# Projection products of 386 columns instead of 392 in a hybrid SSD / DeltaNet / MoE layer

## The reference

```
h = rmsnorm(x, lp['norm1_w']) * (1 + sc1) + sh1
proj = h @ lp['w_in']
xbc = jax.nn.silu(centred_dwconv(xbc, lp['conv_ssd_w'], lp['conv_ssd_b']))    # padding 2 on both sides
qkv = jax.nn.silu(centred_dwconv(qkv, lp['conv_dn_w'], lp['conv_dn_b']))
```

## Time and profile before

| | |
|---|---|
| median of three runs | 1172.71 us (1168.2 to 1173.03) |
| the profiled execution | 1171.63 us |
| its span, first to last instruction | 1169.7 us |
| mean granted TensorE clock | 0.961 |
| TensorE busy | 1037.3 us, 89% |
| VectorE, ScalarE, GpSimd busy | 514.2, 293.9, 228.9 us |
| L734, all 1176 products, in the chain of waits | 18.1% of the span |

### The profile page before, as it was taken

One profiled execution on the slowest core, in us unless ns is written; L12 is line 12 of the kernel. 1 busy time (PEld: TensorE's weight loads), 2 busy tenths in 40 slices (PEclk: granted clock), 3 DMA queues, 4 the chain that ended last, 5 costly groups with the idle time before them and its releaser, 6 DMA issues.

```text
span 1169.7 us, 21559 instructions
## 1 busy us (share of the span) xinstructions
PE 1037.3 (89%) x9055; PEld 679.7 (58%) x9055; DVE 514.2 (44%) x1013; ACT 293.9 (25%) x663; POOL 228.9 (20%) x180
## 2 busy tenths in 40 slices
PE   2799999998898788888999799998988989999895
PEld 1599999997554577778555454443433433444342
DVE  0675776213874455667410433442332333333344
ACT  2432333434452334344100330110111111111112
POOL 0554555561141322322000200000000000000000
PEclk9899999999996999999999899999998999999998
DMA  9742423416052600100412589999999999999993
GB/s 358 255 144 73 144 97 120 144 73 243 10 207 87 253 4 4 40 3 22 144 46 99 214 307 387 407 425 427 425 426 426 424 426 426 426 425 425 426 426 126
DMA packets 54909, 279.11 MB, mean 239 GB/s; under 512 B 6712, under 2 KB 14136, under 8 KB 36016
## 3 DMA queue, kind: packets, MB, share of 16 engines
q1 hardware_dynamic: 51296, 270.12, 57.4%
q0 software_dynamic: 3536, 7.85, 1.8%
HBM read 278.12 MB, written 4.72 MB: 242 GB/s over the span
## 4 chain that ended last, share of the span: by engine, by line
PE 60%; DMA 23%; DVE 10%; ACT 3%; issue 2%; POOL 1%; SPq 1%; DVEq 0%; ACTq 0%
DMA ring_b<-in_w_up 18%; PE ps L734 18%; PE ps L1173 13%; PE ps L1003 7%; DMA ring_a<-in_w_gate 4%; PE ps L1191 2%; PE ps L675 2%; DVE temp L1793 1%; PE ps L824 1%; DMA kv<-in_pos_t 1%; PE ps L926 1%; PE ps L952 1%; PE ps L979 1%; PE ps L804 1%; PE ps L833 1%
## 5 line engine op out<-in xcount | busy, mean ns | idle before, releaser
L734 PE MATMUL ps<-h_hi,w_split 128*128 128x392 f32 x784 | 204.3, 342 | 0.6 <-POOL w_split L584 0.6
L1173 PE MATMUL ps<-ring_b,temp 128*64 128x512 f32 x512 | 124.3, 642 | 28.9 <-DMA ring_b<-in_w_up 28.9
L734 PEld LDWEIGHTS ps<-h_hi,w_split 128*128 128x128 f32 x784 | 143.6, 188 | 3.5 <-issue 2.5
L734 PE MATMUL ps<-h_lo,w_split 128*128 128x392 f32 x392 | 134.2, 342 | 0.0
L584 POOL TENSOR_TENSOR w_split<-ring_a,w_split 128x1024 fp32r<-128x1024 f32 x46 | 114.5, 2489 | 92.3 <-ACT w_split L1309 92.3
L1173 PE MATMUL ps<-ring_a,temp 128*64 128x512 f32 x512 | 114.6, 599 | 7.8 <-DMA ring_a<-in_w_gate 6.9
L1191 PE MATMUL ps<-mix,temp 128*64 128x512 f32 x256 | 112.9, 594 | 2.5 <-issue 0.7
L1191 PE MATMUL ps<-kv,temp 128*64 128x512 f32 x256 | 113.3, 596 | 0.0
L2020 DVE SCALAR_TENSOR_TENSOR temp<-temp,silu_c,ps 128x512 f32<-128x512 f32 x16 | 12.0, 747 | 227.5 <-PE ps L1173 227.5
L1173 PEld LDWEIGHTS ps<-ring_b,temp 128*64 128x64 f32 x512 | 43.7, 147 | 107.9 <-issue 107.9
L1173 PEld LDWEIGHTS ps<-ring_a,temp 128*64 128x64 f32 x512 | 42.6, 139 | 76.7 <-issue 76.5
(11 more groups left out here) (329 smaller groups left out, 1652.3 us busy)
## 6 DMA issues: line engine op xcount, KB each, us to landing
ring_b<-in_w_up SPq DMA_DIRECT2D x30, 2048.0 KB, 18.1
ring_a<-in_w_gate SPq DMA_DIRECT2D x28, 2048.0 KB, 17.3
mix<-in_w_down SPq DMA_DIRECT2D x32, 1024.0 KB, 16.4
kv<-in_w_down SPq DMA_DIRECT2D x32, 1024.0 KB, 18.5
ring_a<-in_w_in SPq DMA_DIRECT2D x11, 2048.0 KB, 7.7
ring_a<-in_w_ada SPq DMA_DIRECT2D x6, 2048.0 KB, 11.4
ring_b<-in_w_ada SPq DMA_DIRECT2D x6, 2048.0 KB, 19.1
ring_a<-in_w_gate SPq DMA_DIRECT2D x16, 512.0 KB, 6.9
```

The lines of the kernel that those rows point to most:

```text
L734: last = nc.tensor.matmul(ps[:, 2 + n % 3, 0:ROW], w[:, k, :], h[:, k, :], start=(k == 0 and x == 0), stop=(k == KD - 1 and x == 2))
L1173: last = nc.tensor.matmul(ps[64 * e:64 * e + 64, 2 + n, :], xg_t[:, k, 64 * e:64 * e + 64], slots[2 * n + e][:, k, :], start=(k == 0), sto ...
```

## The change

The four zero columns between the two sequences become two: the convolution of a sequence needs two zeros behind it and two ahead of it, and the gap's two serve both. The outer zeros, two on each side, are no columns of the product any more: VectorE writes them once into the three PSUM banks, at the columns 0:2 and 388:390, and the products go to the columns 2:388. The convolution reads 386 shifted columns, j to j + 386. `conv_acc` and `ROW_SEGS` follow. The first sequence now begins at column 0 of a row block and the second at 130.

```
-ROW = TOK + 8
-W5 = TOK + 4
-ROW_SEGS = ((2, SEQ + 2), (SEQ + 6, TOK + 6))
+GAP = 2
+ROW = TOK + GAP
+ROW_SEGS = ((0, SEQ), (SEQ + GAP, ROW))
+OUT0, OUT_COLS = GAP, ROW + 2 * GAP
...
-        conv_acc = carve(784, 2, 388)
+        conv_acc = carve(784, 2, ROW)
...
-                last = nc.tensor.matmul(ps[:, 2, 0:ROW], w_split[:, 0, w, k, :], h[:, k, :], ...)
+                last = nc.tensor.matmul(ps[:, 2, OUT0:OUT0 + ROW], w_split[:, 0, w, k, :], h[:, k, :], ...)
...
-                last = nc.tensor.matmul(ps[:, 2 + n % 3, 0:ROW], w[:, k, :], h[:, k, :],
+                last = nc.tensor.matmul(ps[:, 2 + n % 3, OUT0:OUT0 + ROW], w[:, k, :], h[:, k, :],
...
-                nc.scalar.activation(dest[:, 0:SEQ], conv_acc[:, i % 2, 0:SEQ], ACT.Silu)
-                nc.scalar.activation(dest[:, SEQ:TOK], conv_acc[:, i % 2, SEQ + 4:TOK + 4], ACT.Silu).then_inc(conv_out, 1)
+                for (lo, hi), (a, b) in zip(SEGS, ROW_SEGS):
+                    last = nc.scalar.activation(dest[:, lo:hi], conv_acc[:, i % 2, a:b], ACT.Silu)
+                last.then_inc(conv_out, 1)
...
-                            last = nc.scalar.activation(mix[:, i, lo:hi], ps[:, bank, a:b], ACT.Silu)
+                            last = nc.scalar.activation(mix[:, i, lo:hi], ps[:, bank, OUT0 + a:OUT0 + b], ACT.Silu)
...
+            for lo in (0, OUT_COLS - GAP):
+                V.memset(ps[:, 2:5, lo:lo + GAP], 0.0)
             V.memset(silu_c[:, :, :], 0.0).then_inc(silu_zero, 1)
...
-            for lo, hi in ((0, 2), (SEQ + 2, SEQ + 6), (TOK + 6, ROW)):
-                last = V.memset(h1_t[:, :, lo:hi], 0.0)
-            link(last)
+            link(V.memset(h1_t[:, :, SEQ:SEQ + GAP], 0.0))
...
-                link(V.tensor_scalar(c_acc, row[:, 0:W5], col("conv_w", CONV_W * i), col("conv_b", i), ALU.mult, ALU.add))
+                link(V.tensor_scalar(c_acc, row[:, 0:ROW], col("conv_w", CONV_W * i), col("conv_b", i), ALU.mult, ALU.add))
...
-                    ins = V.scalar_tensor_tensor(c_acc, row[:, j:j + W5], col("conv_w", CONV_W * i + j), c_acc, ALU.mult, ALU.add)
+                    ins = V.scalar_tensor_tensor(c_acc, row[:, j:j + ROW], col("conv_w", CONV_W * i + j), c_acc, ALU.mult, ALU.add)
```

More of the change, by code:

```diff
@@ L720, in first_block @@
                         pe.wait_ge(made, k + 1)
-                        last = nc.tensor.matmul(ps[:, 2, 0:ROW], w_split[:, 0, w, k, :], h[:, k, :], start=(x == 0 and k == 0), stop=(x == 2 and k == KD - 1))
+                        last = nc.tensor.matmul(ps[:, 2, OUT0:OUT0 + ROW], w_split[:, 0, w, k, :], h[:, k, :], start=(x == 0 and k == 0), stop=(x == 2 and k == KD - 1))
                 last.then_inc(block_mm, 1)
@@ L1339, in _ @@
                         if 2 <= i <= 4:
-                            last = nc.scalar.copy(mix[:, i, lo:hi], ps[:, bank, a:b])
+                            last = nc.scalar.copy(mix[:, i, lo:hi], ps[:, bank, OUT0 + a:OUT0 + b])
                         else:
-                            last = nc.scalar.activation(mix[:, i, lo:hi], ps[:, bank, a:b], ACT.Silu)
+                            last = nc.scalar.activation(mix[:, i, lo:hi], ps[:, bank, OUT0 + a:OUT0 + b], ACT.Silu)
                     last.then_inc(block_out, 1)
```

## The result

The changed kernel took 1169.31 us, the median of 19 runs (1165.26 to 1173.65), beside 1173.18 us for the kernel before in 19 runs (1168.20 to 1178.77). The ratio is 0.9965, with a 95% interval of 0.995 to 0.998: 4.1 us less, between 2.3 and 5.9. (The two medians are 3.9 us apart, the two means 4.1.) The forecast was 2.9 us less and 1169.8 us.

What follows compares the result with a forecast made beforehand. TensorE's projection products bound the front, DMA the tail that the front starts. 1176 products at 2.5 ns less give 2.94 us, all else nothing, so 1172.71 becomes 1169.8 us; range 1164 to 1175.

Steps and rivals of the forecast that it cites:

- Where the time is set: Projection products (L734): TensorE busy without idle time, nothing else late, so all of the 2.94 us is on the path.
- What six columns are worth: Projection products, 392 to 386 columns: 2.5 ns each, 1176 products, 2.94 us; bounds zero and 3.2 us.
- rival B: Projection's moving rows of 1544 bytes, six of eight starting off 32 bytes: net +11.2 us, 1183.9 us; chance 0.05.
- Everything else at nothing: First block, h1 copies and subtractions, convolution, ScalarE's reads, memsets: nothing on the path.
- The end: DMA-limited tail: expert loads start earlier by as much as the projection ends earlier, so the gain passes through; 1169.8 us.
- A: Projection stage: weight loads set the product spacing, so gain 0 and time 1172.7 us; chance 0.10.
- D: Tail's transfers: mix and kv stand 192 bytes lower, which could lose 5 us, time 1175; chance 0.04.
- C: Low-clock stretches, such as 351 to 371 us, fall elsewhere: 3.9 us each, time 1165.9 or 1173.7; chance 0.16.

Runs made afterwards that it cites:

- The smaller step: Changed kernel with the first product of each of the 49 blocks issued twice, measured twice: medians 1185.01 and 1182.55 us, 12.7 and 13.2 above the changed kernel's.
- TensorE alone: Separate programs without the layer, 72 products of each kind; fp32r at 512 columns 226.7 ns a product, 392 columns at rows of 392 178.8, 386 at rows of 386 176.1.
- the kernel with the old allocation: Changed kernel with h1 rows 392 apart and buf_h at its old size, products still 386 columns: 1169.77 us against 1173.61 for the kernel before, ratio 0.9959.

## Why the prediction was right, step by step

*Where the time is set.* Right. TensorE fills the stage after as before, the weight loads, VectorE, ScalarE and GpSimd being behind it, and 34.4 us added to the stage came out as 36.1. The smaller step, 8.4 and 8.6 us that came out as 12.7 and 13.2, is not explained, so at the size of this change one for one is borne out by the gain itself (3.7 us of stage, 4.1 us between 2.3 and 5.9) and not more closely.

*What six columns are worth.* The sign was right and the size too small, and this is the term that was off. I took 2.5 ns a product and 2.7 as the bound, from two widths, 392 and 512; measured are 3.3 in the long piece, and the stage is 3.7 us shorter where I had 2.94, with 3.2 as the far end. I had read the 16 to 19 ns above the columns' time as a fixed extra with noise on it. They move by up to 5 ns with the width. In the kernel 392 columns carry 15.9 ns above the columns' time, and 386 columns 15.4 at the same row length and 15.1 at the new one. So of the 0.8 ns that I had too little, 0.5 go with the width and 0.3 with the row length, which the prediction priced only as a cost (rival B). The slope to 512 columns could not give this: it was taken from another stream, where 512 columns carried 19 ns, and with TensorE alone they carry 13.3. Why 392 is the dearer of the two in the kernel stays open; TensorE alone at rows of 392 has it the other way round (15.4 and 15.9 ns).

*Everything else at nothing.* Right: the memsets at 0.09 us in front of a wait of 12 us, convolution and copies inside the blocks' cover (VectorE 79.41 of 118.20 us).

*The end.* The three ratios of the changed kernel, 0.9965, 0.9952 and 0.9963, stand for 4.1, 5.6 and 4.3 us, and their intervals all include the stage's 3.7. Forecast and result differ by 0.5 us in the median (1169.8 and 1169.31), less than the runs can tell. That it is so close is in part luck: the gain was forecast 0.9 us too small against the two medians, and the kernel before, 1172.71 us in three runs, came out 0.5 us higher in nineteen.

*Rivals.* A falls by the products with narrow weights and by the spacing itself, which has come down by 3.3 ns. The Trainium skill's figure of 131 ns for 512 columns (TensorE: Matmul & The Clock Gate, section "Back-to-back issue gap") was not seen here either: 226.7 ns with TensorE alone. B falls: the rows of 386 columns, of which six in eight stand off a multiple of 32 bytes, are 0.3 ns a product cheaper in the kernel. But its mechanism is not nothing: with TensorE alone, rows that all start two columns (8 bytes) further cost 1.5 ns a product, under the 3.3 from which B would have decided. D falls by the kernel with the old allocation. C describes how far single executions differ (3.1 us at one place here, 3.9 reckoned); that the changed kernel's low stretch near 709 us is mere chance is not shown, with one profile of the kernel before to set it against.

## What to carry to other kernels

In a stage that TensorE fills without a gap, and whose end starts the rest, every column of every product counts: 1176 products made 3.7 us out of six columns, and the kernel's time went down by about as much. Price a change of width by products at both widths and both row lengths in the same stream, not by a slope from afar, and look for zero or padding columns that can stand in PSUM once instead of passing through every product. A gain of 0.3% is read from the stage's own pieces in the chain, since low-clock stretches elsewhere move a single execution by as much.

## What had not been expected of the hardware

fp32r products with new 128x128 weights start N/2.4 + 13.3 ns apart at 512, 384, 320 and 256 columns, and up to 18 ns over N/2.4 at widths between (396 columns: 183.2 ns, though 400 take 180.1). In the kernel the same width of 384 takes 175.4 ns instead of 173.5, and the two kernels with rows 392 apart and other PSUM columns give the same 118.42 us, so these nanoseconds repeat from program to program. A full row of weight loads beside the products says nothing of a limit: it went from 100% to 62% at one spacing. What in the address or the width sets them stays open.
